# One decoder step on one core: signals per PSUM half in the dense layers, last down weights in free buffers, one product for the sample delta's keys and queries, norms as merged passes

## The reference, cut to what matters

```python
def ffn_half_step(x, w_gate, w_up, w_down, g, b):
    return layer_norm(DEEP_ALPHA * x + 0.5 * swiglu(x, w_gate, w_up, w_down), g, b)
```

```python
def mixer_residual(x, att, gdn, w_o, g, b):
    return layer_norm(DEEP_ALPHA * x + jnp.concatenate([att, gdn], -1) @ w_o, g, b)
```

## Time and profile before

| | |
|---|---|
| median of 3 runs | 3325.1 us (3324.25 to 3327.13) |
| profiled execution | 3333.44 us, span from first to last instruction 3331.7 us |
| mean granted PE clock | 0.932 |
| PE busy | 2891.3 us (87%) |
| DVE busy | 1499.1 us (45%) |
| ACT busy | 871.2 us (26%) |
| POOL busy | 272.3 us (8%) |

### The profile page before, as it was taken

One profiled execution on the slowest core, in us unless ns is written; L12 is line 12 of the kernel. 1 busy time (PEld: TensorE's weight loads), 2 busy tenths in 40 slices (PEclk: granted clock), 3 DMA queues, 4 the chain that ended last, 5 costly groups with the idle time before them and its releaser, 6 DMA issues. The chain is left out here.

```text
span 3331.7 us, 44622 instructions
## 1 busy us (share of the span) xinstructions
PE 2891.3 (87%) x17494; PEld 2622.2 (79%) x17508; DVE 1499.1 (45%) x2239; ACT 871.2 (26%) x1350; POOL 272.3 (8%) x426
## 2 busy tenths in 40 slices
PE   6999999999769999767777488779689999999986
PEld 6999999999558799643777355459489999999984
DVE  3222232232545778448777667442523223332235
ACT  2111111111223467402444244331321111111102
POOL 0000000000000000023422000650000000000000
PEclk8999999999879999759898699999899999999998
DMA  3111111110031122323000200772021111111101
GB/s 113 39 47 46 43 45 44 38 45 13 7 110 39 53 73 78 91 74 93 26 26 7 90 1 1 228 216 69 0 76 40 44 45 45 39 39 48 42 7 54
DMA packets 266530, 186.11 MB, mean 56 GB/s; under 512 B 61727, under 2 KB 246255, under 8 KB 266326
## 3 DMA queue, kind: packets, MB, share of 16 engines
q1 hardware_dynamic: 215478, 114.81, 12.1%
q0 software_dynamic: 20320, 57.28, 5.2%
q10 hardware_dynamic: 30528, 11.15, 1.3%
HBM read 156.96 MB, written 26.22 MB: 55 GB/s over the span
## 5 line engine op out<-in xcount | busy, mean ns | idle before, releaser
L310 DVE TENSOR_TENSOR ffn_hidden<-ffn_hidden,ffn_ps_b 128x1092 f32<-128x1092 f32 x44 | 56.9, 1293 | 406.1 <-PE ffn_ps_b L84 406.1
L293 DVE TENSOR_TENSOR ffn_lo_g<-ffn_raw_g,ffn_hi_g 128x1024 fp32r<-128x1024 f32 x44 | 53.9, 1225 | 349.2 <-ACT ffn_hi_g L258 349.2
L265 ACT ACTIVATE ffn_hi_d<-ffn_raw_d 128x1024 fp32r<-128x1024 f32 x44 | 46.5, 1058 | 549.4 <-PE ffn_ps_b L84 424.0
L280 ACT ACTIVATE ffn_h_hi<-ffn_hidden 128x1092 fp32r<-128x1092 f32 x44 | 49.2, 1119 | 502.4 <-DVE ffn_hidden L310 502.4
L177 POOL DMA_DIRECT2D ffn_raw_d<-in_ffn_w_down x44 | 23.4, 531 | 1793.6 <-DVE ffn_lo_d L299 1581.5
L84 PE MATMUL ffn_ps_a<-mixer_mix_hi,ffn_hi_g 128*128 128x364 f32 x528 | 118.9, 334 | 42.5 <-DVE ffn_lo_g L293 30.0
L84 PE MATMUL ffn_ps_a<-first_x_hi,ffn_hi_g 128*128 128x364 f32 x528 | 119.5, 335 | 24.2 <-DVE first_res L322 12.0
L84 PE MATMUL ffn_ps_a<-ffn_h_hi,ffn_hi_d 128*128 128x364 f32 x528 | 119.9, 336 | 22.6 <-DVE ffn_lo_d L299 18.2
L273 ACT ACTIVATE ffn_hidden<-ffn_ps_a 128x1092 f32<-128x1092 f32 x44 | 47.7, 1083 | 321.7 <-PE ffn_ps_a L84 321.7
L84 PEld LDWEIGHTS ffn_ps_a<-mixer_mix_hi,ffn_hi_g 128*128 128x128 f32 x528 | 92.1, 190 | 45.8 <-DVE ffn_lo_g L293 30.6
L84 PE MATMUL ffn_ps_a<-mixer_mix_lo,ffn_hi_g 128*128 128x364 f32 x528 | 117.9, 330 | 0.7 <-issue 0.6
(11 more groups left out here) (566 smaller groups left out, 7047.4 us busy)
## 6 DMA issues: line engine op xcount, KB each, us to landing
ffn_raw_g<-in_ffn_w_gate SPq DMA_DIRECT2D x44, 512.0 KB, 3.7
ffn_raw_u<-in_ffn_w_up SPq DMA_DIRECT2D x44, 512.0 KB, 3.7
ffn_raw_d<-in_ffn_w_down POOLq DMA_DIRECT2D x44, 512.0 KB, 3.7
proj_raw<-in_w_in SPq DMA_DIRECT2D x22, 512.0 KB, 3.8
scratch_qkv<-proj_stage POOLq DMA_DIRECT2D x12, 544.0 KB, 3.0
delta_cur<-scratch_qkv SPq DMA_DIRECT2D x8, 768.0 KB, 5.4
ats_k_raw<-in_cache_k POOLq DMA_DIRECT2D x96, 64.0 KB, 3.1
ats_k_raw<-in_cache_k SPq DMA_DIRECT2D x96, 64.0 KB, 3.0
```

The source lines that it names most:

```text
L265: act.activation(d_hi[:, k, :], raw["d"][:, :], ACT.Copy).then_inc(whi_done["d"], 1)
L280: act.activation(h_hi[:, par, fb, :], act_buf[:, fb, :], ACT.Copy).then_inc(hhi_done, 1)
L293: dve.tensor_tensor(lo[kind][:, :], raw[kind][:, :], hi[kind][:, :].bitcast(F32), ALU.subtract).then_inc(wlo_done[kind], 1)
L310: dve.tensor_tensor(hid, hid, ps_b[:, :, 0:SL], ALU.mult).then_inc(mul_done, 1)
```

## The change

- `ffn`: the additions of the down products are counted in two semaphores, one for each PSUM half, and a product waits for the additions of its own half. The last chunk's down weights are loaded into the raw gate and up buffers when the last gate and up weights have been split, and split into the high and low gate and up buffers during the preceding down products: on ACT before any of its additions, on DVE ahead of the fifth addition. The first gate and up weights are loaded in the block before: by POOL in `load_tokens`, by SP in the second `norm`.
- `norm`: the deviation step is gone, the root reads PSUM with epsilon as its bias. Per slice DVE runs eight instructions that multiply by `g` and by the reciprocal root, ACT eight that add `b` and round the high part, DVE eight for the low part, tile after tile. `res` keeps its value without `b`. The multiplication by alpha moves to the next user, with alpha times `b`: eight ACT instructions in `mixer_output` ahead of the third weight block's rounding, and eight in the second `ffn` after the first down weights' rounding. The store after the first norm goes out after DVE's product.
- `delta_sample`: keys and queries lie in one buffer and are read in one product of 16 columns, evacuated by one instruction. The decay of the state is split in two, one half behind the subtractions of each level. The state is stored head by head. ACT issues the two table loads that SP issued first.
- `mixer_output`: POOL loads alpha's column and then waits for the first two weight blocks before it issues the residual's loads.

The core of the diff:

```diff
+        @block.gpsimd
+        def _(pool):
+            load_first(pool, raws, w_gate, w_up, sc.sem("first_in"))
...
+def load_first(eng, raws, w_gate, w_up, sem):
+
+    for kind, w in (("g", w_gate), ("u", w_up)):
+        eng.dma_start(raws[kind][:, :].rearrange("p (k f) -> p k f", k=KT),
+                      w[0, :, 0:P].rearrange("(k p) f -> p k f", p=P)).then_inc(sem, 16)
+    eng.wait_ge(sem, 32)
...
-            load(sp, "g", 0, True)
-            load(sp, "u", 0, True)
+            if resid_b is not None:
+                column_load(sp, shift[:, :], resid_b[0], shift_in)
...
+            for k, kind in enumerate("gu"):
+                sp.wait_ge(wlo_done[kind], FB)
+                sp.dma_start(raw[kind][:, :], w_down[0, bass.ts(FB - 2 + k, P), :]).then_inc(raw_in[kind], 16)
...
-            with pool.Fori(1, FB) as n:
+            with pool.Fori(1, FB - 2) as n:
...
-                        pe.wait_ge(down_added, g * 8 - 8)
+                        pe.wait_ge(added_a, g * 4 - 4)
...
+                    if fb == 0 and not first:
+                        pe.wait_ge(added_b, g * 4 - 4)
...
-                pe.wait_ge(wlo_done["d"], d * 2 + 2)
+                if last:
+                    pe.wait_ge(wlo_done["g"], FB + 1)
+                    pe.wait_ge(wlo_done["u"], FB + 1)
+                else:
+                    pe.wait_ge(wlo_done["d"], d * 2 + 2)
                 pe.wait_ge(hlo_done, d * 2 + 2)
                 if last:
-                    pe.wait_ge(down_added, d * 8)
+                    pe.wait_ge(added_a, d * 4)
+                    pe.wait_ge(added_b, d * 4)
...
-                        pe.wait_ge(down_added, d * 8 + m - 1)
+                        pe.wait_ge(added_a if m % 2 == 0 else added_b, d * 4 + m // 2)
...
-                               lambda k: d_hi[:, k, m * P:(m + 1) * P], lambda k: d_lo[:, k, m * P:(m + 1) * P],
+                               lambda k: (hi["gu"[k]] if last else d_hi[:, k])[:, m * P:(m + 1) * P],
+                               lambda k: (lo["gu"[k]] if last else d_lo[:, k])[:, m * P:(m + 1) * P],
...
-            per_chunk(act, gates, lambda d, last: None if last else down_hi(d + 1))
+            if resid_b is not None:
+                act.wait_ge(shift_in, 16)
+                act.activation(shift[:, :], shift[:, :], ACT.Copy, scale=ALPHA).then_inc(shift_made, 1)
+                act.wait_ge(shift_made, 1)
+                for k in range(KT):
+                    act.activation(res[:, k, :], res[:, k, :], ACT.Identity, scale=ALPHA, bias=shift[:, k:k + 1]
+                                   ).then_inc(res_scaled, 1)
+            def down(d, last, one_left=False):
+                if one_left:
+                    for kind in "gu":
+                        act.wait_ge(raw_in[kind], FB * 16)
+                        act.wait_ge(filled[kind], FB)
+                        act.activation(hi[kind][:, :], raw[kind][:, :], ACT.Copy).then_inc(whi_done[kind], 1)
+                elif not last:
+                    down_hi(d + 1)
+
+            per_chunk(act, gates, down)
...
+                    if one_left and m == 4:
+                        weight_lo("g", FB)
+                        weight_lo("u", FB)
...
-                    sp.wait_ge(s["res_done"], i + 1)
+                    sp.wait_ge(s["normed"], KT * (i + 1))
...
+            if early is not None:
+                early(sp, s["early_in"])
...
+            def high(i):
+                for k in range(KT):
+                    act.wait_ge(s["normed"], KT * i + k + 1)
+                    out = res if x_hi is None else x_hi
+                    last = act.activation(out[:, k, cols[i]], res[:, k, cols[i]], ACT.Identity,
+                                          bias=gb[:, 1, k:k + 1])
+                    last.then_inc(s["hi_done"], 1)
...
+                act.wait_ge(s["var_done"], i + 1)
+                act.activation(rstd[:, cols[i]], var[:, i, 0:SL], ACT.Sqrt, bias=eps[:, :]).then_inc(s["std_done"], 1)
...
+                    dve.scalar_tensor_tensor(res[:, k, cols[i]], res[:, k, cols[i]], gb[:, 0, k:k + 1],
+                                             rstd[:, cols[i]], ALU.mult, ALU.mult).then_inc(s["normed"], 1)
...
+                    dve.scalar_tensor_tensor(x_lo[:, k, cols[i]], res[:, k, cols[i]], gb[:, 1, k:k + 1],
+                                             x_hi[:, k, cols[i]].bitcast(F32), ALU.add, ALU.subtract)
...
+            for h in range(GH):
+                sp.wait_ge(s["state_added"], h + 1)
+                sp.dma_start(state_out[:, h].rearrange("b k v -> k b v"), state[:, :, h, :]).then_inc(s["stored"], 16)
...
-                    pe.matmul(b[2][:, h, ts], state[:, i, h, :], k_t[:, h, ts], start=True, stop=True)
-                    last = pe.matmul(b[7][:, h, ts], state[:, i, h, :], q_t[:, h, ts], start=True, stop=True)
+                    last = pe.matmul(reads[:, :, h, ts], state[:, i, h, :], kq_t[:, :, h, ts], start=True, stop=True)
...
+            for dst, src in own_tables:
+                act.dma_start(dst, src).then_inc(s["tables_in"], 16)
...
-            act.activation(ks_t[:, :, :], b[2][:, :, 0:n], ACT.Copy).then_inc(s["reads_copied"], 1)
-            act.activation(qs_t[:, :, :], b[7][:, :, 0:n], ACT.Copy).then_inc(s["reads_copied"], 1)
+            act.activation(read_t[:, :, :, :], reads, ACT.Copy).then_inc(s["reads_copied"], 1)
...
-            own(dve.tensor_tensor(state_rows, state_rows, over_cols(totals[:, :], P), ALU.mult))
...
+                part = slice((l - 1) * DEC_B * GH // 2, l * DEC_B * GH // 2)
+                own(dve.tensor_tensor(state_rows[:, part, :], state_rows[:, part, :], over_cols(totals[:, part], P),
+                                      ALU.mult))
...
+            column_load(pool, shift[:, :], resid_b[0], s["shift_in"])
+            for par in range(2):
+                pool.wait_ge(s[f"raw_in{par}"], 48)
...
+            def scale_residual():
+                act.wait_ge(s["shift_in"], 16)
+                act.activation(shift[:, :], shift[:, :], ACT.Copy, scale=ALPHA).then_inc(s["shift_made"], 1)
+                act.wait_ge(s["shift_made"], 1)
+                act.wait_ge(s["res_in"], 16 * KT)
+                for k in range(KT):
+                    act.activation(res[:, k, :], res[:, k, :], ACT.Identity, scale=ALPHA, bias=shift[:, k:k + 1]
+                                   ).then_inc(s["res_scaled"], 1)
+
             for m in range(KT):
+                if m == 2:
+                    scale_residual()
...
-            dve.wait_ge(s["res_in"], 16 * KT)
+            dve.wait_ge(s["res_scaled"], KT)
```

112 lines of the change are left out of this document (48 added, 64 removed).

## The result

The changed kernel takes 3230.06 us (median of four, 3220.45 to 3234.84) against 3325.78 us (four, 3324.25 to 3327.13): a ratio of 0.970, 95% interval 0.9687 to 0.9713. That is 95.7 us less; the forecast was 97.3 less.

What follows compares the result with a forecast made beforehand. TensorE is busy nine tenths or more in the dense layers, so time can come only from its idle stretches or its work; eight terms sum to 97.3 us off the median 3325.1, giving 3227.8, range 3209 to 3246.

Steps and rivals of the forecast that it cites:

- A: First dense layer's start: gate and up weights loaded beside the token rows gain 2.2 us, between 0.6 and 3.7.
- E: Sample delta: fewer read products 12.9, decay hidden 3.0, smaller last store 5.0, earlier loads 0.6; 21.5 us (18 to 23).
- G: Second norm and second layer's start: norm 5.0, preloaded weights 3.7, residual scaling priced at nothing; 8.7 us (3 to 14).
- B: Dense layers: a signal per PSUM half removes PE's waits for additions before gate products; 24.5 us (22 to 26).
- C: Each dense layer's last down product: weights through free gate and up buffers remove idling and lower clock; 19.8 us.
- D: First norm: merged narrow passes, eight taking 4.24, and the store hidden under the low parts; 11.6 us (8 to 17).
- F: Output projection: residual held until two weight blocks land, start 8.6 earlier less a stall of 1.1; net 7.4 us.
- H: Third norm: deviation step gone, multiply plus scaling replaced by eight passes and one ACT instruction; 1.6 us (-1 to 3).
- 1 and 2: Rivals in the norms: eight narrow passes take 4.8, total 3236, chance 0.11; or 3.3, total 3214, chance 0.08.
- 3: Rival: moved transfers and ACT passes find no cover; 8 us lost, total 3236, chance 0.08.
- 4 and 5: Rivals: last down product still waits, 3248, chance 0.03; PE's clock drops inside the dense layers, slower, chance 0.02.

Runs made afterwards that it cites:

- run 9: Changed kernel, but both dense layers load their first gate and up weights at their own start; first gate product at 40.72 us, no total time given.
- run 1: Changed kernel, but a gate product following a down product waits again for the last additions of both PSUM halves; 3254.81 us, ratio 0.9777.
- run 7: Changed kernel, but norms multiply each third in one wide VectorE instruction, ScalarE applying scale and shift; third norm 54.1 us for 47.0, no total time given.
- run 8: Changed kernel, but GpSimd issues the residual without waiting, with the shift column ahead or behind; output projection stretch 111.4 and 114.1 us for 110.2, no total time.
- two_reads: Changed kernel, but keys and queries in sample delta multiply each state block in two products of 8 columns again; 3246.97 us, ratio 0.9758.
- run 4: Changed kernel, with the up weights' subtraction moved behind a down product's second addition and the last down product's other-half wait moved to its second output; 3214.0 us.
- run 5: Kernel of run 4, with TensorE's loop over chunk pairs in the dense layers written out straight; 3210.76 us, ratio 0.965.
- run 10: Kernel of run 4 plus the projection's first two weight blocks loaded during the first norm, 3212.3 us; that preload on run 5's kernel with memsets moved later, 3204.74 us.

## Why the prediction was right

3228 was forecast, 3230 measured. The mechanisms forecast for A to E and for G are there, and undone one at a time they give back 3.0 (A), 25.6 (B), 20.7 (C), 5.5 (the store of D), 13.6 (the reads of E) and 6.4 (the weights of G). F's was half wrong. That the number came within 2 us is in part luck, as the end of this section says. The gains below are those between the two profiled executions.

- **A** 2.2, measured 3.1 (3.0 in run 9). The first gate product comes anywhere from 36.5 to 39.5 in the traces with the preload, so this is near the forecast, and no more than that. The Trainium skill (Trainium Kernel Development and Optimization, Key Constraints) has the issues of all queues run on the same DMA engines and interleave. The worst bound that the forecast drew from this, 0.6, is not what the runs show: the weights beside the rows cost little.
- **B** 24.5, measured 31.0 (19.2 and 11.8 over the passages of run 1's table). The mechanism was right; the idle time was the wrong measure: a passage went from 50.30 to 48.51, 1.79 for 1.39, and run 1 shows where most of the 0.4 lies. Eighteen stops of 1.39 are 25.0, eighteen times 0.4 some 7 more, two long passages of the profiled execution of before add 3.4 (51.52 and 52.51), and the four loop turns take 4.5 away. The two long ones were misread in the earlier trace rows: the 12.0 of the first layer is not nine stops of 1.39 but seven, and one of 2.26 behind which the clock fell to its lower level (a granted 0.51 from 390.0 to 392.5); the ninth, of 2.62, names no engine and stands there under "issue":

```profile
240.80 0.76 PE L84 MATMUL ffn_ps_a<-first_x_hi,ffn_hi_g 128*128 128x364 f32 x3 [2.62 <-issue]
```

- **C** 19.8, measured 9.3 and 10.6, 20.0, clock and waits as forecast.
- **D** 11.6, measured 10.4. The first mean products ran at a lower granted clock in this execution of after and not in that of before, 1.7 us (last section); at equal clocks it is 12.1. The store's share is 5.5 to 5.9 for 6.6. From the first reciprocal to the last low part it is 38.2 for the forecast 39.2; a pass of eight takes 4.08 to 4.16 for 4.24. What the merging itself is worth in D, G and H is read from the two traces; run 7 undoes the split multiply alone.
- **E** 21.5, measured 22.3: reads 13.6 for 12.9, decay 3.0 for 3.0, store 5.5 for 5.0, and issue order 0.2 for 0.6. The stage's first products do come 1.1 sooner behind its first issue, but the reads wait for the state, which was issued 0.95 sooner and took 0.73 longer. Decay, store and issue order are read from the two traces too; no run undoes them.
- **F** 7.4, measured 6.9. The sum was right and the cause half wrong: the forecast gave the whole earlier start to POOL's wait. By run 8 the wait gives 2.9 at the start, which the later residual takes back; the column ahead of the residual, priced at nothing but its own 0.4, gives 3.1. That the sum came out owes something to luck.
- **G** 8.7, measured 9.5, at equal clocks (both norms start at the lower level). The residual's scaling on ACT is covered: PE has no wait behind it. The preload's 3.7 holds against the kernel before; inside the changed kernel it is worth 6.4, because its new column load would have stood in front.
- **H** 1.6, measured 5.5: 1.7 of it clock again (the other way), 1.9 in the store of the tokens, and 2.0 the change's own. The store is not the change's: `two_reads`, with the code of after, takes 24.7 there like the execution of before (24.6), and the other traces take 22.7. In these two DVE waits some 3 us for a buffer that a transfer still reads; why stays open.

The rivals: 1 and 2 fell by the pace, 3 by A, F and G, 4 and 5 by the clock and the wait of C.

The eight places together give 108.7 between the two traces, 11.4 more than forecast, and the stretches without an edit take 3.8 back. Some 7 of this is the one execution of before: the two long passages (3.4), the third norm's clock (1.7) and the store (1.9). It lay 7.7 above its median, and so the medians, which the forecast named, are only 95.7 apart. B's restarts and its loop turns, neither of which the forecast had, offset each other in part as well. So the 2 us are partly luck. Taken singly, the terms of A, C, D, E, F and G are right to about 1 us, and B was 3 too small even without that execution's long passages.

## What to carry to other kernels

When a wait on another engine's last result is taken away, ask at once what is late next on that engine and on the one that waited. Here the loop's turn came out from under the removed waits, and memsets came out from under a removed transfer; a subtraction in front of the first addition had been there all along. Mending these, with the projection's first weights loaded ahead, was worth 12.8 us in run 4, 5.4 in run 5 and 4.7 at the projection's start in run 10. Price a removed PE stop by the spacing of whole passages rather than by the idle time alone. When an edit makes one thing start sooner by holding another back, follow the one held back to where it is needed. And a small load is not free because it is small: what it stands in front of, or holds back, decides.

## What the runs showed of the hardware that was not expected

**The clock at a stage's start.** The norms' first mean products, behind the same 2.1 to 2.2 us of idle PE, run at the full clock in some executions and not in others: 5.2 or 6.9 us to the first centring. Windows from the first mean product on, norms one and three of the kernel after and norm three of the kernel before:

```profile
840.80:847.70 6.90, 6.85 (x17) 4.24 (x18) 0.06 (x1) 0.00 (x0) 0.00 (x0) 0.75 0.16 1
...
3157.00:3162.20 5.20, 5.18 (x17) 3.33 (x18) 0.07 (x2) 0.00 (x0) 0.00 (x0) 1.00 0.21 2
...
3256.40:3263.30 6.90, 6.82 (x17) 4.11 (x18) 0.00 (x0) 0.00 (x0) 0.00 (x0) 0.75 0.17 4
```

In the kernel before it was the second and the third norm that had 0.75, and the first 1.00. Over the fourteen profiled executions 15 of the 42 norms start so. What decides it stays open; it moves a stretch by 1.7 us, which is as much as some terms above.

**The loop's turn.** It stops PE in the second layer, where a passage gets 1.0 to 1.3 us longer, and not in the first, with the same code (run 5).

**Narrow passes.** Eight passes over 364 columns on ACT take 4.16 us with one per-row operand and 4.76 with two (D and run 7); on DVE eight with a per-row scalar and two tensors take 4.16 (D).

**A stop costs more than its idle time.** 1.48 us of idle PE in a run of matmuls cost 1.7 (run 1).
